# Moving the SBUF tensors of a one-core decoder layer to other addresses modulo 512 bytes

## What is computed

```python
h = modulate(rms_norm(x, gains[0]), ...)
x = x + 0.5 * gate1 * swiglu(h, ffn1_w_in, ffn1_w_down)         # 1024 -> 2 x 2816 -> 1024
h = modulate(rms_norm(x, gains[1]), ...)
(hq, hf, hi, hg, gq, gk, gv, gg, g_low, r_hg, r_gla) = split(h @ w_in_mix)
y_hg  = hgrn2_branch(hq, hf, hi, hg, ...)                       # 4 heads, 128 x 128 states
y_gla = gla_branch(gq, gk, gv, gg, g_low, ...)                  # 4 heads, 64 x 128 states
x = x + gate2 * ((sigmoid(r_hg) * (y_hg @ w_up_hg) + sigmoid(r_gla) * (y_gla @ w_up_gla)) @ w_out)
h = modulate(rms_norm(x, gains[2]), ...)
x = x + 0.5 * gate3 * swiglu(h, ffn2_w_in, ffn2_w_down)
out = rms_norm(x, final_norm)
```

## Time and profile before

| | |
|---|---|
| median of three runs | 1182.98 us |
| the profiled execution | 1181.76 us |
| its span, first to last instruction | 1179.9 us |
| TensorE busy | 1152.3 us, 98% of the span |
| TensorE weight loads busy | 1030.7 us, 87% |
| VectorE busy | 781.9 us, 66% |
| ScalarE busy | 507.7 us, 43% |
| GpSimd busy | 90.6 us, 8% |
| mean granted TensorE clock | 0.996 |

### The profile page before, as it was taken

How to read it: one execution, slowest core, us unless ns; L and a number is a source line. 1 busy time by engine, 2 the same in 40 slices (tenths; PEclk the granted TensorE clock), 3 DMA queues, 4 the chain that set the end, 5 groups by cost and what they waited for, 6 DMA issues and landing times.

```text
span 1179.9 us, 18541 instructions
## 1 busy us (share of the span) xinstructions
PE 1152.3 (98%) x7385; PEld 1030.7 (87%) x7385; DVE 781.9 (66%) x1061; ACT 507.7 (43%) x646; POOL 90.6 (8%) x137
## 2 busy tenths in 40 slices
PE   6999999999999999999999999999999999999997
PEld 5789999998889997878787888888999999998887
DVE  5788888777877577666463446756868887863222
ACT  6455554552122456555244322234445545442322
POOL 2000000002220122222010001000000000000000
PEclk9999999999999999999999999999999999999999
DMA  9423333337885131122211457442223333333321
GB/s 353 158 98 107 107 107 107 107 122 268 305 282 165 37 108 39 37 71 75 75 65 37 146 176 248 145 143 72 72 72 107 107 107 107 107 98 98 98 63 72
DMA packets 115126, 143.51 MB, mean 122 GB/s; under 512 B 4084, under 2 KB 102784, under 8 KB 115072
## 3 DMA queue, kind: packets, MB, share of 16 engines
q1 hardware_dynamic: 106800, 113.32, 29.5%
q0 software_dynamic: 8064, 29.36, 7.2%
q10 hardware_dynamic: 208, 0.08, 0.0%
HBM read 140.65 MB, written 2.10 MB: 121 GB/s over the span
## 4 chain that ended last, share of the span: by engine, by line
PE 88%; DVE 7%; ACT 3%; issue 1%; DMA 1%; SPq 0%; DVEq 0%; ACTq 0%
PE PS L819 29%; PE PS L575 16%; PE PS L577 16%; PE PS L576 16%; PE PS L898 1%; PE PS L934 1%; PE PS L904 1%; PE PS L620 1%; PE PS L622 1%; PE PS L621 1%; PE PS L733 1%; DVE ACC L1751 1%; DMA ADA<-in_w_ada_dram 1%; DVE ACC0a L1762 1%; ACT WH L1127 1%
## 5 line engine op out<-in xcount | busy, mean ns | idle before, releaser
L1649 DVE TENSOR_TENSOR WL<-RAW,WH 128x2048 fp32r<-128x2048 f32 (+2 forms) x55 | 120.5, 2191 | 129.1 <-ACT WH L1127 128.9
L575 PE MATMUL PS<-HH,WH 128*128 128x512 f32 (+2 forms) x488 | 185.4, 380 | 5.6 <-DVE HL L1677 3.2
L1127 ACT ACTIVATE WH<-RAW 128x2048 fp32r<-128x2048 f32 (+2 forms) x55 | 100.6, 1828 | 195.2 <-PE PS L577 188.7
L577 PE MATMUL PS<-HH,WL 128*128 128x512 f32 (+2 forms) x488 | 177.1, 363 | 0.0
L576 PE MATMUL PS<-HL,WH 128*128 128x512 f32 (+2 forms) x488 | 176.5, 362 | 0.0
L819 PE MATMUL PS<-HH,WH 128*128 128x256 f32 x576 | 161.3, 280 | 0.6 <-DVE WL L1936 0.6
L819 PE MATMUL PS<-HL,WH 128*128 128x256 f32 x576 | 161.0, 279 | 0.0
L819 PE MATMUL PS<-HH,WL 128*128 128x256 f32 x576 | 160.7, 279 | 0.0
L575 PE MATMUL PS<-UH,WH 128*128 128x512 f32 (+1 forms) x416 | 147.0, 353 | 0.0
L577 PE MATMUL PS<-UH,WL 128*128 128x512 f32 (+1 forms) x416 | 146.2, 351 | 0.0
L576 PE MATMUL PS<-UL,WH 128*128 128x512 f32 (+1 forms) x416 | 145.4, 350 | 0.0
(11 more groups left out here) (320 smaller groups left out, 2239.9 us busy)
## 6 DMA issues: line engine op xcount, KB each, us to landing
RAW<-in_ffn_w_in_dram SPq DMA_DIRECT2D x42, 1024.0 KB, 5.1
ADAW<-in_w_ada_dram POOLq DMA_DIRECT2D x56, 512.0 KB, 5.5
RAW<-in_w_in_mix_dram SPq DMA_DIRECT2D x22, 1024.0 KB, 5.2
RAW<-in_ffn_w_down_dram SPq DMA_DIRECT2D x16, 1024.0 KB, 5.1
ADA<-in_w_ada_dram SPq DMA_DIRECT2D x16, 512.0 KB, 10.6
RAW<-in_ffn_w_down_dram SPq DMA_DIRECT2D x7, 768.0 KB, 4.4
RAW<-in_w_out_dram SPq DMA_DIRECT2D x3, 1024.0 KB, 5.7
XST<-in_x_dram SPq DMA_DIRECT2D x4, 512.0 KB, 5.3
```

Source lines behind the costliest of these rows:

```text
L575: mm(ps, whi, ahi, start=start, stop=False)
L577: return mm(ps, wlo, ahi, start=False, stop=stop)
L1127: A(WH[slot(n)][:, 0:size], RAW[slot(n)][:, 0:size], ACT.Copy).then_inc(unit_hi, 1)
L1649: V.tensor_tensor(WL[s][:, 0:size], RAW[s][:, 0:size], WH[s][:, 0:size].bitcast(F32), ALU.subtract)\
```

## The change

A tensor FRONT of 384 bytes is put ahead of X. X, RAW, WH, WL, S and PT so move up by 384 bytes, from phase 128 to phase 0. PST leaves its place behind PT and is placed in the arena at offset 86528, right behind MASKF (86016 to 86528); the tables after it so move down by 128 bytes. The arena's base is moved from phase 192 to phase 0; its address falls from 89792 to 89600. Nothing else is changed: no instruction, no size, no semaphore, no transfer is added or taken away, and FRONT is neither read nor written. No other tile has data in those 512 bytes while PST is in use.

```diff
+        sb("FRONT", [P, 96])
         X = sb("X", [P, DB, T])
         RAW = [sb(f"RAW{s}", [P, UNIT]) for s in range(2)]
         WH = [sb(f"WH{s}", [P, UNIT], F32R) for s in range(2)]
         WL = [sb(f"WL{s}", [P, UNIT], F32R) for s in range(2)]
         S = sb("S", [P, T])
         PT = sb("PT", [P, 124])
-        PST = sb("PST", [124, P])
...
         MASKF = place("MASKF", [P, P], 86016)
+        PST = place("PST", [124, P], 86528)
...
     size = arena.shape[1] * 4
     start = (nc.sbuf_base - size) // 32 * 32
-    return start + (192 - start) % 512
+    return start + -start % 512
```

## The result

The changed kernel takes 1189.19 us (median of seven runs, 1188.54 to 1192.02), the kernel before 1183.62 us in the same comparison (seven runs, 1181.11 to 1185.51). The ratio is 1.0052 with a 95% interval of 1.0039 to 1.0064: slower by 0.5%, about 6 us. The direction is the one that was forecast, the size is not: +15 us were forecast.

A forecast was written before the change was run, and what follows sets the result against it. The prediction took TensorE, through the distance between matmul starts, to bound the kernel. 8.5 + 4.8 + 1.7 = +15.0 us on 1182.98 gave 1198 us, own range 1185 to 1205, with 1163 to 1205 us to hold 8 in 10.

The forecast's parts named there:

- The bound and how to read it: Whole kernel: TensorE, 88% of the chain, sets the time through the distance between matmul starts, not through waits.
- The step from the earlier trace to all 256-column matmuls: 3864 matmuls of 256 columns go from 117.8 to 120.0 ns, the value of equal phases in `last_unit`: +8.5 us.
- `unit_v`: Its 384 matmuls go from a mix of 113.4 and 117.8 to 120.0 ns: +1.7 us, between 0 and +2.5.
- `last_unit`, ScalarE and VectorE: 168 matmuls keep equal phases: 0; the two engines' new operand addresses taken as 0, at most 1.0 us either way.
- The long pieces: Two unbroken chain pieces of 1428 matmuls each in the seven products grow from 168.6 to about 171.8 us each.
- the term of 512 columns: 2184 matmuls of 512 columns go one step up from 228.9 ns, to 231 ns: +4.8 us.
- the other bound: 2184 matmuls of 512 columns go one step down, to 226.7 ns: -4.8 us.
- the terms cancel: 256 columns lose 2.2 ns, 512 columns gain it: +5.4 us, 1188 us; counted within the forecast's slower case, 0.50.
- a loss once for each load and not along the columns: 512-column matmuls: the condition given for the distance falling to 226.7 ns, -4.8 us.
- the first 80 us: Start of the kernel: a sign, to stay the same within 1 us in the profile after.
- The fast value in both forms: 256 columns go to 113.4 ns, 512 columns down two steps: -28.5 us, 1154 us; the faster case's chance 0.34.
- Addresses do nothing: All matmuls: phases 0 and 0 act as 128 and 192 did, no change, 1183 us; chance 0.16.

The follow-up runs named there:

- w128_a128: Changed kernel with FRONT left out and the arena at phase 128, so X, RAW and weights are at 128 too: 1188.72 us, ratio 1.0048 to the kernel before.
- w0_a64: Changed kernel with the arena at phase 64 instead of 0, X, RAW and weights staying at 0: 1183.6 us, ratio 1.0002 to the kernel before.
- w0_a256: Changed kernel with the arena at phase 256 instead of 0, X, RAW and weights staying at 0: 1187.93 us, ratio 1.0037 to the kernel before.
- mixm64b: Changed kernel, FRONT out, 256-column weights 192 bytes below the arena's phase, other units at equal phase, splits placed where TensorE reads: 1173.65 us, ratio 0.993.
- light: Kernel before, with splits in the second down projection cut to 64 of 2048 columns from its third unit on: 1184.58 us, a single execution.
- mix kernels: Changed kernel, FRONT out; 256-column weights 32, 192 or 64 bytes below the arena's phase, other units at equal phase: 1180.86, 1174.65 and 1181.7 us.
- w0_a448: Changed kernel with the arena at phase 448 instead of 0, X, RAW and weights staying at 0: 1191.06 us, ratio 1.0045 to the kernel before.
- mixm64: Changed kernel, FRONT out, 256-column weights 192 bytes below the arena's phase, other units at equal phase, some values not the layer's: 1174.65 us, ratio 0.9933.
- mix64: Changed kernel, FRONT out, 256-column weights 64 bytes below the arena's phase, other units at equal phase, some values not the layer's: 1181.7 us, ratio 0.9982.
- w0_a32: Changed kernel with the arena at phase 32 instead of 0, X, RAW and weights staying at 0: 1189.33 us, ratio 1.0059 to the kernel before.

## Why the prediction was wrong

**What held.** The bound and how to read it: no other engine's busy time moved by more than 0.2 us, of TensorE's waits the longest went from 9.2 to 8.5 us and the others by at most 0.3, and the time went with the distance between matmuls. The step from the earlier trace rows to all 256-column matmuls held to the number: 120.0 ns, +7.8 us where +8.5 was forecast (the step between the long pieces is 2.14 ns and not 2.2, and a part of the 3864 lies behind interruptions, where the distance is not the free one). `unit_v` went to 120.0, +1.5 for +1.7. `last_unit`, ScalarE and VectorE did not move, as costed. The long pieces were forecast at 171.8 us and are 171.66. That equal phases at 192 stand for equal phases at 0 was shown by w128_a128 and w0_a64. Read as streamed minus loaded, the three pairs of the kernel before were +64, 0 and -64, and for 256 columns each already showed what its difference gave in the later runs: 117.8 (nearly everywhere), 120.0, and 113.3 or 117.8 ns.

**The step that failed** is the term of 512 columns: "I take one step up, as for 256 columns: +4.8 us, between the two and nearer to the upper, which has been seen." It was one step down, 226.7 ns and -3.6 us. This one term is 8.4 us of the 9 us by which the forecast was off. The true distance was the other bound that I had written (-4.8 us there and -3.6 measured: between interruptions the step is smaller, 231.1 to 229.7 ns in the 48 matmuls from 341 us, 345 us after), and the case itself stood among the rivals as "the terms cancel", at +5.4 us and 1188 us; the four classes came to +5.7. I took the upper because the earlier trace rows showed 233.0 ns. But those rows were taken at a difference of +64, right after an interruption, and said nothing about a difference of 0; a value that has been seen under another condition was given the weight of a nearest row. What had been argued for the lower bound, a loss once for each load and not along the columns, is what the numbers at 0 look like: the step from 256 to 512 columns is 226.7 - 120.0 = 106.7 ns there, and 256 periods of the granted 2.4 GHz are 106.7 ns as well, so nothing is left that grows with the columns. At +64 the step is 228.9 - 117.8 = 111.1 ns, so there a part of the loss does grow with them. That 512 columns move the way that 256 do was the wrong assumption.

A sign that missed: the first 80 us were to be the same within 1 us. In the profiled pair the first long piece starts at 90.53 us instead of 88.97, 1.6 us later, which goes with the clock (see w0_a256). The prediction read the clock as high in every slice and had no term for when it rises.

**The rivals.** The fast value in both forms did not come at 0. It is real for 256 columns only, at -64 and in one stretch at +64, and gave the 1173.65 us of mixm64b. "Addresses do nothing" is refuted: 16.5 us lie between +64 and +96 with the same instructions. With it falls the time that the prediction drew from the rule of the Trainium skill in "SBUF — State Buffer", section "Who interferes with whom", by which TensorE's two read ports are independent and it waits for nobody: addresses did change the distance. Whether what is lost is a wait at a port, no run shows. The rule does fit `light` in so far as it concerns other engines: without their splits the distance was the same. What is left are TensorE's own two operands.

**What stays open.** By which mechanism the two operands' reads lengthen a matmul. That the pattern repeats after 256 bytes is measured for 0 and 256 in whole kernels, and for +32, +64 and -64 inside the mix kernels. The steps of 2.2 ns that the prediction saw hold between 117.8 and 120.0 and between 226.7 and 228.9 ns, but 116.7, 118.6 and 118.9 ns do not stand on them. That two streams meet in the same part of the memory is an argument. So is what picks one of two values: no run shows it. The start, +2.5 us of matmul distances in the profiled pair, goes by the clock as far as the rows show, and was not isolated.

## What to carry to other kernels

Where TensorE never waits, read the distance between the starts of its matmuls, for each form, in every tile pair that the trace has: two pairs that differ only in addresses are an experiment that has already been run. In this kernel the address of the streamed operand minus that of the loaded one, modulo 256 bytes as far as tried, was worth 1.5% of the time, the best value differed between forms (0 for 512 columns, +32 or -64 for 256), and an offset of 8 or 48 floats inside the weight tile gave each form its own and won 0.4 or 0.7%. A difference with two values has to be run many times: one execution of mixm64b says little about the next. A term without a row of its own condition should keep both of its bounds open in the sum, instead of leaning to the one that was seen under another.

## What the runs showed of the hardware that was not expected

- Matmuls of fp32r weights and columns follow each other at 113.3, 116.7, 117.8, 118.6 or 120.0 ns for 256 columns and at 226.7, 228.9 or 232 to 234 ns for 512, with the same instructions at other addresses; other differences give values up to 120.2 ns between these.
- At a difference of -64 there are two lasting values for 256 columns, 113.3 and 117.8 ns (w0_a448, mixm64, mixm64b, and `unit_v` of the kernel before). At +64 they are 117.8 ns nearly everywhere, and 113.3 in one stretch of light. At 0 every free stretch, in three kernels, is at 120.0.
- In the first 30 us loads into SBUF ran faster where the rows start at a multiple of 256 bytes. Packets of 2048 bytes took 84.1 ns in the mean with the arena at 0 and 84.2 at 256, but 88.8 at 192, 88.4 at 128 (w128_a128) and 87.5 or 87.6 at 64 and 448; those of 1024 bytes into RAW took 46.0 ns with RAW at phase 0 and 50.7 at 128. Over the whole execution the latter are 50.0 and 50.7 ns, with a median of 46 in both. From 10 to 20 us the core took 403 GB/s after the change and 382 before. In executions with the late clock the first long piece started at 90.53 us with the arena at 0 and at 256, and at 91.08 (mix64, phase 192) to 91.94 us (w0_a32) elsewhere. The matmul distances differ between these as well, so how much of the start belongs to the loads is open, and the median times don't resolve it.
